# Routing weights of the expert layers as two reduced-precision products, with the one-hots of four tokens made in one pass

## The reference

```python
def block(xb):
    q = (xb @ w_q).reshape(PEER_BLOCK, PEER_HEADS, 2, PEER_DHALF)
    s = jnp.einsum('thpd,hpkd->thpk', q, subkeys).astype(jnp.float32)
    s1, i1 = lax.top_k(s[:, :, 0], PEER_TOPK)
    s2, i2 = lax.top_k(s[:, :, 1], PEER_TOPK)
    ...
    top, pos = lax.top_k(cand, PEER_TOPK)
    idx = jnp.take_along_axis(cidx, pos, axis=-1)
    g = jax.nn.softmax(top, axis=-1)
    ue, ve = u[idx], v[idx]
    act = jax.nn.gelu(jnp.einsum('td,thkd->thk', xb, ue).astype(jnp.float32), approximate=False)
    return jnp.einsum('thk,thkd->td', (g * act).astype(xb.dtype), ve)
```

## Time and profile before

| | |
|---|---|
| median of 3 runs | 5324.82 us (5319.91 to 5328.98) |
| the profiled execution's own time | 5323.69 us |
| its span | 5322.0 us, 72934 instructions |
| mean granted TensorE clock | 0.917 |
| TensorE busy | 4621.6 us (87%) |
| VectorE busy | 3122.0 us (59%) |
| ScalarE busy | 2266.6 us (43%) |
| routing products of layer 0 | 964.5 to 1424.8 us |
| routing products of layer 1 | 2817.6 to 3021.3 us |

### The profile page before, as it was taken

One profiled execution on the slowest core, in us unless ns is written; L12 is line 12 of the kernel. 1 busy time (PEld: TensorE's weight loads), 2 busy tenths in 40 slices (PEclk: granted clock), 3 DMA queues, 4 the chain that ended last, 5 costly groups with the idle time before them and its releaser, 6 DMA issues. The chain is left out here.

```text
span 5322.0 us, 72934 instructions
## 1 busy us (share of the span) xinstructions
PE 4621.6 (87%) x25788; PEld 3882.1 (73%) x25788; DVE 3122.0 (59%) x7266; ACT 2266.6 (43%) x4298; POOL 6.3 (0%) x20
## 2 busy tenths in 40 slices
PE   7768899999999999776899999788858798874978
PEld 2446788888878888545899977578638788862977
DVE  7545688555444444425787677655575555556555
ACT  6423333666533333213448755444324444423444
POOL 0000000000000000000000000000000000000000
PEclk9889999999999999887999999889859899985989
DMA  8400444455656666201566788544204335420343
GB/s 303 151 26 32 141 129 133 163 181 182 208 185 189 190 189 186 72 33 63 179 216 230 262 264 267 187 169 151 81 0 166 146 146 185 149 67 12 154 158 146
DMA packets 355500, 810.27 MB, mean 152 GB/s; under 512 B 29864, under 2 KB 171304, under 8 KB 335508
## 3 DMA queue, kind: packets, MB, share of 16 engines
q1 hardware_dynamic: 355224, 806.79, 45.0%
HBM read 704.87 MB, written 101.81 MB: 152 GB/s over the span
## 5 line engine op out<-in xcount | busy, mean ns | idle before, releaser
L170 DVE TENSOR_TENSOR w_low__6<-w_raw,w_high__6 128x512 fp32r<-128x512 f32 x544 | 362.0, 688 | 440.7 <-ACT w_high__6 L165 440.3
L158 PE MATMUL hidden<-hT_high,w_high__6 128*128 128x512 f32 x1152 | 456.7, 396 | 15.3 <-DVE w_low__6 L170 15.3
L160 PE MATMUL hidden<-hT_high,w_low__6 128*128 128x512 f32 x1152 | 450.8, 391 | 0.0
L159 PE MATMUL hidden<-hT_low,w_high__6 128*128 128x512 f32 x1152 | 449.0, 390 | 0.0
L170 DVE TENSOR_TENSOR w_low__11<-w_raw__2,w_high__11 128x512 fp32r<-128x512 f32 x544 | 362.6, 689 | 122.2 <-ACT w_high__11 L165 106.8
L165 ACT ACTIVATE w_high__6<-w_raw 128x512 fp32r<-128x512 f32 x544 | 324.2, 624 | 216.8 <-PE side L160 204.4
L165 ACT ACTIVATE w_high__11<-w_raw__2 128x512 fp32r<-128x512 f32 x544 | 321.8, 624 | 70.9 <-PE side__2 L160 35.6
L158 PE MATMUL hidden__3<-hT_high__2,w_high__11 128*128 128x256 f32 x1152 | 331.8, 288 | 11.3 <-DVE w_low__11 L170 11.3
L160 PE MATMUL hidden__3<-hT_high__2,w_low__11 128*128 128x256 f32 x1152 | 327.4, 284 | 0.0
L159 PE MATMUL hidden__3<-hT_low__2,w_high__11 128*128 128x256 f32 x1152 | 327.1, 284 | 0.0
L158 PEld LDWEIGHTS hidden<-hT_high,w_high__6 128*128 128x128 f32 x1152 | 217.2, 189 | 58.3 <-DVE w_low__6 L170 15.6
(11 more groups left out here) (1034 smaller groups left out, 12746.1 us busy)
## 6 DMA issues: line engine op xcount, KB each, us to landing
w_raw<-in_peer_u SPq DMA_DIRECT2D x128, 512.0 KB, 3.8
w_raw<-in_peer_v SPq DMA_DIRECT2D x128, 512.0 KB, 3.8
w_raw__2<-in_peer_u SPq DMA_DIRECT2D x128, 512.0 KB, 4.0
w_raw__2<-in_peer_v SPq DMA_DIRECT2D x128, 512.0 KB, 4.9
activated_dram<-activated SPq DMA_DIRECT2D x128, 256.0 KB, 4.1
routing_dram<-routing SPq DMA_DIRECT2D x32, 1024.0 KB, 6.2
routing_chunk<-routing_dram SPq DMA_DIRECT2D x16, 2048.0 KB, 10.7
activated_again<-activated_dram SPq DMA_DIRECT2D x128, 256.0 KB, 4.1
```

The costliest lines, as they stand in the source:

```text
L158: nc.tensor.matmul(out, lhs[0], rhs[0], start=start, stop=False, skip_group_check=True)
L159: nc.tensor.matmul(out, lhs[0], rhs[1], start=False, stop=False, skip_group_check=True)
L160: return nc.tensor.matmul(out, lhs[1], rhs[0], start=False, stop=stop, skip_group_check=True)
L170: return nc.vector.tensor_tensor(low, src, high.bitcast(F32), ALU.subtract)
```

## The change

`one_hots` makes both one-hots, i and j, of all four tokens in a single is_equal over 2 x 4 x 128 elements (`hots`), waits for it, and multiplies the one-hots of j with the high and the low part of the weights in one more pass over 2 x 4 x 128 (`oj`). Both tiles have the type F32R. `route` makes two products for each token, one-hot of i by high part and by low part, which accumulate. ScalarE's `last_one_hot` goes; its fourth copy in `keep_picks` makes the high part of the weights instead of minus i, and VectorE makes the low part once a layer (`gain_parts`). The ring of one-hots has four groups instead of eight.

```diff
--- before.py
+++ after.py
@@ -873,7 +873,7 @@
     NT = len(tiles)
     N = NT * P
     U = 2 * NT
-    RR, RB, AHEAD, AR, AD, RS = 3, 4, 3, 6, 4, 8
+    RR, RB, AHEAD, AR, AD, RS = 3, 4, 3, 6, 4, 4
     iota, iota16 = consts["iota"], consts["iota16"]
 
     UP, DOWN = 2 * H + PE_K, PE_K
@@ -934,11 +934,11 @@
         cand2 = arena.at(32 * KB, "pair_rest", [P, U, K * K])
         same = arena.at(24 * KB, "same", [P, V, U, K, K])
         keys = arena.at(40 * KB, "subkeys", [P, 2 * H, PE_K])
-        oi = arena.at(0, "one_hot_i", [P, RS, 4, P])
-        oj = arena.at(16 * KB, "weight_at_j", [P, RS, 4, P])
-        off = arena.at(32 * KB, "distance", [P, RS, P])
-        staged = arena.at(36 * KB, "routing", [P, 2, PE_K, GT])
-        minus_i = arena.at(52 * KB, "minus_i", [P, N])
+        hots = arena.at(0, "one_hots", [P, RS, 2, 4, P], F32R)
+        oj = arena.at(16 * KB, "weight_at_j", [P, RS, 2, 4, P], F32R)
+        staged = arena.at(32 * KB, "routing", [P, 2, PE_K, GT])
+        g_high = arena.at(48 * KB, "gain_high", [P, N], F32R)
+        g_parts = arena.at(50 * KB, "gain_parts", [P, 2, N])
         G = arena.at(0, "routing_chunk", [P, 2, NC, JC, GT])
         weighed = arena.at(32 * KB, "weighed", [P, 2, N])
         w_high = arena.at(36 * KB, "weighed_high", [P, 2, N], F32R)
@@ -955,11 +955,11 @@
         G_loaded = st.sems_of("routing_loaded", 2)
         gate_loaded = st.sems_of("gate_rows_loaded", len(gate_rows))
         (keys_loaded, high_ready, split, used, evacuated, scored, kept, ranked, own, centred, exp_done, selected,
-         turned, picked, distances, last_hot, hot, product, staged_in, weighed_ready, weighed_high, weighed_split,
+         turned, picked, hot, product, staged_in, weighed_ready, weighed_high, weighed_split,
          done) = (st.sem(x) for x in (
              "keys_loaded", "pieces_high_ready", "pieces_split", "pieces_used", "hidden_evacuated", "scores_ready",
              "scores_kept", "scores_ranked", "dve_wrote", "centred", "exp_done", "selected", "picks_turned",
-             "picks_kept", "distances_ready", "last_one_hots_ready", "one_hots_ready", "routing_ready",
+             "picks_kept", "one_hots_ready", "routing_ready",
              "routing_staged", "weighed_ready", "weighed_high_ready", "weighed_split", "sum_kept"))
         block = st.begin()
 
@@ -1046,14 +1046,16 @@
 
             def route(g):
                 pe.wait_ge(hot, g + 1)
-                pe.wait_ge(last_hot, g + 1)
                 if g >= 4:
                     pe.wait_ge(staged_in, g - 3)
                 else:
                     pe.wait_ge(picked, 4)
                 for k in range(4):
-                    last = nc.tensor.matmul(side[:, g % 4, k * P:(k + 1) * P], oi[:, g % RS, k, :], oj[:, g % RS, k, :],
-                                            start=True, stop=True)
+                    out = side[:, g % 4, k * P:(k + 1) * P]
+                    nc.tensor.matmul(out, hots[:, g % RS, 0, k, :], oj[:, g % RS, 0, k, :], start=True, stop=False,
+                                     skip_group_check=True)
+                    last = nc.tensor.matmul(out, hots[:, g % RS, 0, k, :], oj[:, g % RS, 1, k, :], start=False,
+                                            stop=True, skip_group_check=True)
                 last.then_inc(product, 1)
 
             def combine(d):
@@ -1119,18 +1121,7 @@
                 act.wait_ge(turned, 1)
                 for k in range(3):
                     nc.scalar.activation(picks[:, k, :], side[:, k, 0:N], ACT.Copy).then_inc(picked, 1)
-                nc.scalar.activation(minus_i[:, :], side[:, 0, 0:N], ACT.Copy, scale=-1.0).then_inc(picked, 1)
-
-            def last_one_hot(g):
-                if g == 0:
-                    act.wait_ge(picked, 4)
-                if g >= RS:
-                    act.wait_ge(product, g - RS + 1)
-                nc.scalar.activation(off[:, g % RS, :], iota, ACT.Abs, bias=minus_i[:, 4 * g + 3:4 * g + 4]) \
-                    .then_inc(distances, 1)
-                act.wait_ge(distances, g + 1)
-                nc.scalar.activation(oi[:, g % RS, 3, :], off[:, g % RS, :], ACT.Relu, scale=-1.0, bias=1.0) \
-                    .then_inc(last_hot, 1)
+                high_part(nc, g_high[:, :], side[:, 2, 0:N]).then_inc(picked, 1)
 
             def stage(g):
                 k = g // 4
@@ -1170,9 +1161,6 @@
                     weighed_high_part(s - UP + 1)
                 if s + AHEAD < SLOTS:
                     make_high(s + AHEAD, 1)
-                for g in range(NG):
-                    if route_at[g] == s:
-                        last_one_hot(g)
                 if s < UP:
                     evacuate(s)
 
@@ -1291,18 +1279,26 @@
                                                    total[:, t].unsqueeze(2).broadcast_to([P, H, K]), ALU.mult)
                 last.then_inc(selected, 1)
 
+            def gain_parts():
+                dve.wait_ge(picked, 4)
+                nc.vector.tensor_copy(g_parts[:, 0, :], g_high[:, :].bitcast(F32))
+                chain.wrote(nc.vector.tensor_tensor(g_parts[:, 1, :], picks[:, 2, :], g_high[:, :].bitcast(F32),
+                                                    ALU.subtract))
+
             def one_hots(g):
                 if g == 0:
-                    dve.wait_ge(picked, 4)
+                    gain_parts()
                 if g >= RS:
                     dve.wait_ge(product, g - RS + 1)
-                t = 4 * g
-                nc.vector.tensor_tensor(oi[:, g % RS, 0:3, :], iota.unsqueeze(1).broadcast_to([P, 3, P]),
-                                        picks[:, 0, t:t + 3].unsqueeze(2).broadcast_to([P, 3, P]), ALU.is_equal)
-                for k in range(4):
-                    last = nc.vector.tensor_scalar(oj[:, g % RS, k, :], iota, picks[:, 1, t + k:t + k + 1],
-                                                   picks[:, 2, t + k:t + k + 1], ALU.is_equal, ALU.mult)
-                last.then_inc(hot, 1)
+                t, r = 4 * g, g % RS
+                chain.settle()
+                chain.wrote(nc.vector.tensor_tensor(
+                    hots[:, r], iota.unsqueeze(1).unsqueeze(1).broadcast_to([P, 2, 4, P]),
+                    picks[:, 0:2, t:t + 4].unsqueeze(3).broadcast_to([P, 2, 4, P]), ALU.is_equal))
+                chain.settle()
+                nc.vector.tensor_tensor(
+                    oj[:, r], hots[:, r, 1].bitcast(F32).unsqueeze(1).broadcast_to([P, 2, 4, P]),
+                    g_parts[:, :, t:t + 4].unsqueeze(3).broadcast_to([P, 2, 4, P]), ALU.mult).then_inc(hot, 1)
 
             def weigh(d):
                 dve.wait_ge(act_loaded[d % AD], 16 * (d // AD + 1))
```

## The result

Twenty runs of each kernel: 5327.1 us before (5319.91 to 5334.27), 5338.5 us after (5331.84 to 5344.21). The ratio is 1.002 with the interval [1.0013, 1.0027]: 11.4 us slower, 0.21%, at the edge of what counts here as a difference: the prediction draws the line at 0.2%, and the interval reaches to both sides of it.

What follows compares the result with a forecast made beforehand. TensorE was taken to bound both routing stretches, with VectorE's spare room wide in the first layer, narrow in the second. 0 (TensorE) + 10.1 (VectorE) + 0 (rest) = +10 us, median 5324.8 to 5334.8; range 5320 to 5349.

Steps and rivals of the forecast that it cites:

- case A: Whole kernel, the main forecast: products keep their price, VectorE overruns the second layer; 5320 to 5344 us, chance 0.70.
- TensorE's price, 0 us: Routing products in both layers: each record stays at 0.1117 us, the weight load seeming the limit; 0, ends -48 and +114.
- B: Rival, routing products: a narrow product takes the streaming price of 65 ns; together -39 us, 5286, chance 0.11.
- C: Rival, routing products: the 256-column rows' 120 ns are a floor of the type; +18.6 us, 5343, chance 0.09.
- D: Rival, routing products: below 256 columns a product costs fp32's 223 ns; +114 and +57 us, 5496, chance 0.10.
- VectorE's group, 2.39 us: VectorE's two one-hot passes per group of four tokens: 1.22 + 0.04 + 1.13 = 2.39 us, 0.89 more than before.
- The second layer, +10.1: Second expert layer's routing stretch: VectorE's work of 215.9 us exceeds 203.7 by 12.2; less 2.1, +10.1 us.
- the lead: Second layer: VectorE finishes a group 2.1 us before TensorE uses it, which comes off the 12.2 us overrun.
- gain_parts, 0 to +1: VectorE, before each layer's first group: two passes once a layer, some 1 us, hidden by the head start; 0 to +1.
- ScalarE: Two activations a group go, worth nothing while TensorE or VectorE is late: 0, from 0 to -1 us.
- the ring: One-hot buffers, four groups instead of eight: a group waits for the product four groups earlier, finished well ahead; 0.
- gain_high: ScalarE's copy making the high part of the weights replaces the minus i copy of like size; 0.

Runs made afterwards that it cites:

- half tiles: Kernel after the change, each token's second product halved: 64 stationary columns in the first layer, 64 moving columns in the second; 5312.1 us in one run.
- plain bfloat16 run: Kernel after the change, with one-hots, weighted one-hots and high part of the weights in bfloat16, layout unchanged; 5275.95 us, ratio 0.9915 to the kernel before.

## Why the prediction was right

**The result.** 5334.8 was forecast on a time before of 5324.8, so +10.0; measured were +11.4, and 5338.5 lies in the range. It fell where the threshold of 0.2% cuts through case A, just on the slower side of it, with an interval that holds both sides. The forecast time lies on the other side, and which side it would be the prediction left open (0.40 to 0.49).

**TensorE's price, 0 us.** Right. The records stayed 111 ns apart, the slot 7.28 us and the first stretch 460.3. The reason given, that the load is the limit, was read from the 8-column rows and the load rows. The half tiles confirm it from both sides: of the two it is the stationary side that moves the time. Rivals B, C and D fall with it in this kernel: no 65 ns, no floor of 120, no 223. B's price exists in bfloat16; in this kernel's type the load rows rightly spoke against it. The line through the 512- and 256-column rows was near the mark for the streaming (65 ns; 0.06 us lie between the first two records of a slot), but streaming is not the limit.

**VectorE's group, 2.39 us.** Right to the hundredth: 1.25 and 1.14 between the starts, as put together from the earlier trace rows. In the first layer 1.20 us of idle time were left in a slot, where 1.2 were forecast, and 74.0 us in all, where 75 were; the run with the change in this layer alone confirms that it is free.

**The second layer, +10.1.** The mechanism is the forecast one, shown three ways: the waits for weight_at_j in exactly the twelve slots with two groups, the run with a shorter pass that takes the loss away, and the run with a product less that does not. The size came out at +11.1 in the stretch (214.8 against a forecast of 213 to 214). VectorE's chain of 215.9 us was met, but by some luck: the sum has one pair of low parts too many (1.2 us) and puts idle time and gaps at nothing (1.2 us), and the two cancel. What was wrong is the lead, the term of 2.1 us. VectorE starts 2.76 us ahead of the first product, but the stretch also runs on 1.5 us behind its last pass, which the prediction did not count, so only 1.2 us come off. The lead had been read in the middle of the layer, in a slot where VectorE had caught up, and not at the start and at the end.

**gain_parts, 0 to +1, "inside the lead".** The bound was right and the place was wrong. There is hardly a lead at the start: the first group is ready at 2817.57 and used at 2817.85. A delay there is a delay of VectorE's whole chain, so its 0.66 us count in full, by reading; no run took them away while the long passes stayed.

**ScalarE, the ring, gain_high at 0.** For the ring, shown: with the ring of 4 and the old routing the second layer has its old 203.6 us. ScalarE's two activations are gone in the run with the short pass too, and its stretch is 204.0, so their going gained nothing there; gain_high was not tested by itself.

**Not foreseen.** The fall to the 1.2 GHz level in the first slot. It cost TensorE some 1.5 us, but by reading no more than 0.8 of the result: VectorE worked on and stood idle only once in the stretch, for 0.8 us, in the slot behind it, and the next slot with two groups lost 0.41 instead of 0.84. The run with one product bears it out: with five such falls its second stretch is 212.7 us. In a stretch that TensorE does not bound, a slow TensorE is cheap.

## What to carry to other kernels

Before a change moves work to an engine that is not the bottleneck, add up that engine's whole work in each stage against the stage's length. Here the same edit is free where VectorE had 189 us of idle time and costs the full overrun, 12 us less the head start, where it had 44. To count the overrun, follow the late engine's chain from its first to its last instruction, with what stands in front of it and what comes after it. And where a small product is bound by the load of its weights, halving its moving columns is worth nothing: use fewer stationary columns, another type or fewer products.

## What the runs showed of the hardware

- Records with a load of 128 stationary columns each start every 111 ns in fp32 and in its reduced type (load record 192 ns), and every 56 ns in bfloat16 (98 ns). With 64 stationary columns in the reduced type it is some 60 ns (138 ns). Where a load was made ahead, the next record of the reduced type started 0.06 us later.
- In bfloat16 a moving operand with a step of four elements (8 bytes) costs 118 ns a record of 128 columns, with a step of two 57 to 58, without a step 56. The same step of four in the stationary operand lengthened the load's record to 113 ns and left the distance between records at 56.
- VectorE's pass over 1024 elements takes 1219 ns with fp32 sources and 685 to 692 with bfloat16 throughout, also where the operands are broadcast with two or four adjacent elements innermost. With output and one source in bfloat16 and the other source in fp32 it stays at 1219 to 1241.
- GpSimd takes 1546 ns for a product over 512 bfloat16 elements (the factors in fp32), and a VectorE pass over 1024 elements with fp32 sources that starts while it works 2.06 us instead of 1.21.
- The granted clock fell to 0.50 for some 3.4 us within 1.6 us after TensorE had waited inside a dense stretch, but the length of the wait does not tell when. In after it fell after the first of twelve waits (1.17 us; the others were at most 0.63), and the same with half tiles (1.20 us, at most 0.66); with one product after five of twelve (1.36 to 1.65 us), not after seven (1.36 to 1.74); in the plain bfloat16 run only after the last of twelve (1.78 us), not after the first (1.56) nor after ten of 1.77 to 1.78. What decides stays open.
